# Phase boundaries of a transformer kernel: squares and gates at the eviction, a diagonal product as the turn, and k-tile pairs turned between units

## The chip, the cores and the metric

The kernel runs on one core of a Trainium2 chip. The metric is the time of one execution on the device in microseconds. A smaller number is better. The core's engines are TensorE (PE; its weight loads are PEld), VectorE (DVE), ScalarE (ACT), GpSimd (POOL) and SyncE (SP, which here only issues loads). Each engine carries out its own instructions in order, and the engines meet through semaphores.

## What is computed

Two transformer blocks on 256 latent tokens and 256 context tokens of width 2048, in fp32. The first block mixes the tokens (an mLSTM and a differential attention), projects, adds, and runs an FFN of width 5632 with a convolution over the tokens, on the latent tokens alone. The second block has two layers with two kinds of attention each; both layers read all 512 tokens, and the last updates the latent ones only. Every residual sum is followed by an RMS norm, a scale and a shift (both from a modulation row that is itself a product of a vector with a large matrix), and a product with a large weight matrix. What matters here is the chain from one large product to the next:

```python
def first_block(...):
    mod = jax.nn.silu(c) @ w_mod[l] + b_mod[l]
    sh1, sc1, ga1, sh2, sc2, ga2 = jnp.split(mod[:, None, :], N_MOD, axis=-1)
    ...
    p_lat = modulate(rmsnorm(x, g_pre_mix[l]), sh1, sc1) @ w_in[l]
    ...
    y_lat = jnp.concatenate([m_lat, d_lat], axis=-1).astype(x.dtype) @ w_out[l]
    x = x + ga1 * rmsnorm(y_lat, g_post_mix[l])
    h_lat = modulate(rmsnorm(x, g_pre_ffn[l]), sh2, sc2)
    x = x + ga2 * rmsnorm(conv_ffn(h_lat, w_up[l], conv_ffn_w[l], conv_ffn_b[l], w_down[l]), g_post_ffn[l])
    ...
def second_block(...):
    for l in range(DEPTH_2):
        h_lat = rms_norm(x, norm_g[l]) * (1.0 + scale[:, None]) + shift[:, None]
        h_ctx = rms_norm(xc, norm_g[l]) * (1.0 + scale_c) + shift_c
        ...
        x = x + gate[:, None] * merge_groups(o_a, lat_a[3], o_b, lat_b[3], w_out[l])
        if l < DEPTH_2 - 1:
            ...
            xc = xc + gate_c * merge_groups(oc_a, ctx_a[3], oc_b, ctx_b[3], w_out[l])
    return rms_norm(x, final_g)
```

## The kernel before

**Tiles and units.** Tokens lie on the 128 partitions: tiles 0 and 1 are latent, tiles 2 and 3 context. A large product is a sequence of groups, each 512 output columns wide (a few are 288), and a group is a sequence of units of two k-tiles, 128 rows of the weight matrix each. SP loads each unit's weights, 512 KB, into one of seven raw slots (L2276). ScalarE rounds them to fp32r as w_hi (L2288), VectorE subtracts to get w_lo (L2309), in four slots of each. TensorE then makes three fp32r products for each pair of operand and weight parts (L2357 to L2359 for 512 columns, L2367 to L2369 where the FFN's up projection keeps the weights still and moves 256 token columns). Units of kind "F" are modulation sums: VectorE multiplies and accumulates 128x1024 slices of the modulation matrices (L630). They are hosted between the units of other groups and share the raw slots.

**Phases and stages.** The program is a list. `gemms` appends a phase, whose steps are the units in order; `stage` appends work that isn't a large product. `walk` runs the list on each engine. Between all entries stands `barrier`: every engine adds to a semaphore, and waits for all four. In a phase `split_and_leave` walks over the steps on ScalarE and VectorE: it makes the split of each unit and, five units after a group's last unit or at the end of the phase, the group's leave, which evacuates its PSUM banks (L852 and L860 copy, 128x512 each). There are eight banks, and a group takes two or four. `AHEAD` = 2 units of the next phase are split inside a stage (`fill`), and their loads run ahead through the raw slots.

**From product to product.** At the end of the out projection and of the FFN's down projection, `after_block` makes the residual of both latent tiles: squares of y (L1803), an rsqrt of twelve small dependent VectorE instructions (L377 to L383), gate and scale (L1812), add (L1814), and a store of x to `x_spill` in DRAM from GpSimd's queue. `norm_stage` follows: squares of X (L729), a second rsqrt, X scaled in place by its reciprocal root (L751, after the spill has read it), 16 k-tiles turned by `transpose` on TensorE against an identity (L770, into four banks in turn), and for each k-tile scale and shift per partition on ScalarE (L737), the rounding to fp32r (L718 on GpSimd for odd k, L758 on VectorE for even), and the remainder (L759). The next phase's `ready` lets TensorE start on a k-tile as soon as its remainder is there, but its first unit comes behind all transposes in TensorE's order. In the layers of the second block, `res_dve` evacuates the out projection: gate (L2151) and add (L2152), per tile, and `res_act` does nothing. Between the FFN's up and down projection stands `stage(pe=wait_prods)`, which waits for the last product of gate and value (L1875 to L1878, after the convolution L1304 and L1307). At the end `fin_act` squares the two tiles (L2183), `fin_dve` makes the rsqrt and scales (L2190), and `fin_pool` stores.

## Time and profile before

| | us |
|---|---|
| three runs | 3493.6, 3494.18, 3501.28 |
| median | 3494.18 |
| the profiled execution | 3489.78 |
| its span on the core | 3488.0 |
| TensorE busy in it | 3064.1 (88%) |
| VectorE, ScalarE, GpSimd busy | 2224.8, 1213.4, 132.5 |
| mean clock granted to TensorE | 0.938 of full |

TensorE is busy in 88% of the span, and its matmuls are recorded with overlapping ends, so a busy TensorE is not one at its peak. In a timeline row the first number is the start, the second the duration, and the bracket behind it says how long the engine had been idle and what released it; for consecutive matmuls the distance of two starts tells what one costs. The granted clock is a share of full speed: 1.0 is 2.4 GHz, 0.5 is 1.2 GHz.

### The profile page before, as it was taken

The page shows a single profiled execution, that of the slowest core. Times are in us where ns is not written, and L with a number is a line of the kernel's source. Part 1 is how long each engine was busy: PE and PEld are TensorE (multiplying, and loading weights), DVE is VectorE, ACT ScalarE, POOL GpSimd, SP SyncE. Part 2 cuts the span into 40 slices and gives each one's busy share as a digit, 9 for nine tenths or more (in the row PEclk, how much of TensorE's full clock was granted, in tenths as well). Part 3 has the DMA queues.
Part 4 walks back from the last instruction along what each step waited for, and adds up shares of the span by engine and source line. Part 5 has one row for each costly group of instructions (what it writes and reads, how often), then busy time and mean ns, then how long its engine had stood idle before and what let it go on. Part 6 is the DMA issues. An engine that isn't in the chain of part 4 may idle for free. (4 is left out here: it accounts for less than half of the span.)

```text
span 3488.0 us, 41971 instructions
## 1 busy us (share of the span) xinstructions
PE 3064.1 (88%) x16281; PEld 2532.7 (73%) x16281; DVE 2224.8 (64%) x3193; ACT 1213.4 (35%) x1751; POOL 132.5 (4%) x198
## 2 busy tenths in 40 slices
PE   5999789996969999998996999888898979978996
PEld 2587567875769999997885888666656767866665
DVE  5768545738757778876866677935347844584354
ACT  6631324313444443433334222124242133324342
POOL 1000000001010000000001000000000000000000
PEclk9999999997989999999998999889999989989998
DMA  7876034730837666667873555521205626661233
GB/s 259 290 253 224 3 106 137 250 136 1 298 125 249 220 233 237 208 227 247 267 241 129 180 175 188 181 85 37 97 1 205 207 84 207 188 209 57 97 121 103
DMA packets 255286, 589.20 MB, mean 169 GB/s; under 512 B 21945, under 2 KB 30369, under 8 KB 250480
## 3 DMA queue, kind: packets, MB, share of 16 engines
q1 hardware_dynamic: 245760, 544.54, 47.2%
q0 software_dynamic: 8928, 41.32, 3.3%
q8 instruction: 129, 2.11, 0.2%
q10 hardware_dynamic: 400, 0.66, 0.1%
q14 instruction: 69, 0.57, 0.1%
HBM read 571.72 MB, written 14.72 MB: 168 GB/s over the span
## 5 line engine op out<-in xcount | busy, mean ns | idle before, releaser
L2288 ACT ACTIVATE w_hi<-raw 128x1024 fp32r<-128x1024 f32 (+1 forms) x732 | 741.8, 1032 | 1388.9 <-PE bank L2359 765.0
L2309 DVE TENSOR_TENSOR w_lo<-raw,w_hi 128x1024 fp32r<-128x1024 f32 (+1 forms) x732 | 858.9, 1190 | 507.1 <-ACT w_hi L2288 503.8
L630 DVE SCALAR_TENSOR_TENSOR acc<-raw,sc_t,acc 128x1024 f32<-128x1024 f32 x480 | 601.0, 1279 | 51.0 <-DMA acc<-in_b_ada 32.9
L2357 PE MATMUL bank<-w_hi,l_hT_hi 128*128 128x512 f32 (+1 forms) x1056 | 399.0, 378 | 46.6 <-DVE w_lo L2309 46.1
L2367 PE MATMUL bank<-f_hT_hi,w_hi 128*128 128x256 f32 x1408 | 407.1, 289 | 29.2 <-DVE w_lo L2309 29.0
L2368 PE MATMUL bank<-f_hT_lo,w_hi 128*128 128x256 f32 x1408 | 405.6, 288 | 0.0
L2369 PE MATMUL bank<-f_hT_hi,w_lo 128*128 128x256 f32 x1408 | 405.3, 288 | 0.0
L2358 PE MATMUL bank<-w_lo,l_hT_hi 128*128 128x512 f32 (+1 forms) x1056 | 395.1, 374 | 0.0
L2359 PE MATMUL bank<-w_hi,l_hT_lo 128*128 128x512 f32 (+1 forms) x1056 | 394.7, 374 | 0.0
L2367 PEld LDWEIGHTS bank<-f_hT_hi,w_hi 128*128 128x128 f32 x1408 | 277.4, 197 | 33.9 <-DVE w_lo L2309 31.6
L2369 PEld LDWEIGHTS bank<-f_hT_hi,w_lo 128*128 128x128 f32 x1408 | 277.8, 197 | 0.0
L2368 PEld LDWEIGHTS bank<-f_hT_lo,w_hi 128*128 128x128 f32 x1408 | 277.3, 197 | 0.0
L2357 PEld LDWEIGHTS bank<-w_hi,l_hT_hi 128*128 128x128 f32 x1056 | 203.5, 193 | 89.5 <-DVE w_lo L2309 46.1
L2359 PEld LDWEIGHTS bank<-w_hi,l_hT_lo 128*128 128x128 f32 x1056 | 203.4, 193 | 33.5
L2358 PEld LDWEIGHTS bank<-w_lo,l_hT_hi 128*128 128x128 f32 x1056 | 204.0, 193 | 32.5
L2357 PE MATMUL bank<-w_hi,b_hT_hi 128*128 128x512 f32 x512 | 204.6, 400 | 20.2 <-DVE w_lo L2309 19.9
L2358 PE MATMUL bank<-w_lo,b_hT_hi 128*128 128x512 f32 x512 | 202.0, 395 | 0.0
L2359 PE MATMUL bank<-w_hi,b_hT_lo 128*128 128x512 f32 x512 | 201.6, 394 | 0.0
L2357 PE MATMUL bank<-w_hi,l_cat_hi 128*128 128x512 f32 x384 | 153.4, 399 | 11.2 <-DVE w_lo L2309 10.6
L2359 PE MATMUL bank<-w_hi,l_cat_lo 128*128 128x512 f32 x384 | 151.7, 395 | 0.0
L2358 PE MATMUL bank<-w_lo,l_cat_hi 128*128 128x512 f32 x384 | 151.7, 395 | 0.0
L2357 PE MATMUL bank<-w_hi,f_a_hi 128*128 128x512 f32 x352 | 139.6, 397 | 10.4 <-DVE w_lo L2309 10.4
(436 smaller groups left out, 4652.3 us busy)
## 6 DMA issues: line engine op xcount, KB each, us to landing
raw<-in_w_in SPq DMA_DIRECT2D x240, 512.0 KB, 4.8
raw<-in_w_mod SPq DMA_DIRECT2D x192, 512.0 KB, 5.3
raw<-in_w_ada SPq DMA_DIRECT2D x192, 512.0 KB, 4.5
raw<-in_w_up SPq DMA_DIRECT2D x176, 512.0 KB, 5.1
raw<-in_w_out SPq DMA_DIRECT2D x96, 512.0 KB, 4.9
raw<-in_w_down SPq DMA_DIRECT2D x88, 512.0 KB, 5.3
raw<-in_w_in SPq DMA_DIRECT2D x32, 288.0 KB, 3.4
raw<-in_w_ukv SPq DMA_DIRECT2D x16, 512.0 KB, 3.7
```

The source lines that it names most:

```text
L630: e.scalar_tensor_tensor(acc[a][:, :], raw[s % RAW_SLOTS][:, :], scalar, acc[a][:, :], ALU.mult, ALU.add).then_inc(fma_done, 1)
L2288: e.activation(slot(w_hi[u % SPLIT_SLOTS], g.width), slot(raw[s % RAW_SLOTS], g.width), ACT.Copy).then_inc(hi_ready, 1)
L2309: e.tensor_tensor(slot(w_lo[u % SPLIT_SLOTS], g.width), slot(raw[s % RAW_SLOTS], g.width), slot(w_hi[u % SPLIT_SLOTS], g.width).bitcast(F3 ...
L2357: e.matmul(o, xh[:, k, tok], hi[:, kk, :], start=first, stop=False)
L2358: e.matmul(o, xh[:, k, tok], lo[:, kk, :], start=False, stop=False)
L2359: mm = e.matmul(o, xl[:, k, tok], hi[:, kk, :], start=False, stop=last)
L2367: e.matmul(o, hi[:, kk, c], xh[:, k, 0:n], start=first, stop=False)
L2368: e.matmul(o, hi[:, kk, c], xl[:, k, 0:n], start=False, stop=False)
L2369: mm = e.matmul(o, lo[:, kk, c], xh[:, k, 0:n], start=False, stop=last)
```

## The change

Five places of the program change. They are the boundaries between the out projection and the FFN's up projection (A), up and down projection (B), down projection and layer 0 (C), layer 0 and layer 1 (D), and the end (E).

- **No barrier and no stage at A to D.** Two phases now follow each other directly. `fill=3` splits the next phase's first three units on ScalarE and VectorE ahead of the last group's leave, and `prev` tells TensorE of which groups of the phase before it must see the banks evacuated.
- **Gate and square at the eviction.** `gated_group` (A, C) multiplies by the gate on VectorE as it evacuates a bank, while ScalarE squares the other tile's bank into a free bank, with the sum over the row; then the two change over. `residual` makes the rsqrt, and then four halves of u times reciprocal root plus X as one instruction each, with a square of each half behind it on ScalarE. At D the squares of x ride on the eviction in `res_act`, one 512-column square for each tile and group.
- **A diagonal product as turn.** X is no longer scaled. `norm_join` writes for each tile the diagonal matrix of its reciprocal roots (`dg`, identity times a column), and TensorE multiplies X's 128x128 block with it, as a plain fp32 matmul (L744 after): the block comes out turned and scaled.
- **Pairs between units.** TensorE turns the k-tiles in eight pairs. Pairs 0, 1 and 2 stand ahead of the next phase's unit 0, and pair q from then on ahead of unit q - 2. Scale and shift, rounding and remainder of pairs 0 and 1 stand ahead of the first step, those of pair q at step q + 1 of ScalarE, GpSimd and VectorE.
- **B** has `ready_prods`: a unit of the down projection waits for its own products of gate and value instead of for all.
- **The context tokens** of layer 0 are loaded during the last group of the down projection (from its unit 11), and squared by ScalarE at its units 18 and 20.
- **Order in the layers.** The key and value group (all four tiles, 24 matmuls a unit) comes ahead of the two query groups.
- **The end.** The final gain is multiplied in at the eviction (`zf`); the reciprocal root is applied in halves of 1024 columns, tile 0 on VectorE, tile 1 on ScalarE; SP stores four pieces of 512 KB.

```diff
@@ -691,103 +707,93 @@
...
+            def turn_pe(q):
+                def pe(e):
+                    e.wait_ge(norm_x, xb + nt)
+                    for k in (2 * q, 2 * q + 1):
+                        if k >= 4:
+                            e.wait_ge(norm_aff, kb + k - 3)
+                        for t in range(nt):
+                            mm = e.matmul(banks[b0 + k % 4][:, P * t:P * t + P], X[:, t, P * k:P * k + P], dg[:, t, :],
+                                          start=True, stop=True)
+                        mm.then_inc(norm_tr, 1)
+                return pe
+            def affine_act(q):
+                def act(e):
+                    for k in (2 * q, 2 * q + 1):
+                        e.wait_ge(norm_tr, kb + k + 1)
+                        if k >= 4:
+                            e.wait_ge(norm_split, kb + k - 3)
+                        for a, b, c in segs:
+                            last = e.activation(tmp[:, k % 4, a:b], banks[b0 + k % 4][:, a:b], ACT.Identity,
+                                                bias=modv[:, v_shift, k, c:c + 1], scale=modv[:, v_scale, k, c:c + 1])
+                        last.then_inc(norm_aff, 1)
+                return act
...
+            def hooks(steps):
+                def parts(at):
+                    yield "act", 0, pre["act"]
+                    yield "dve", 0, diag_dve
+                    yield "pool", 0, pre["pool"]
+                    for q in range(KT // 2):
+                        yield "pe", at(group0, max(q - 2, 0)), turn_pe(q)
+                        later = 0 if q < 2 else at(group0, 7) + 1 if q == 7 else at(group0, q + 1)
+                        yield "act", later, affine_act(q)
+                        yield "pool", later, cast_pool(q)
+                        yield "dve", later, split_dve(q)
+                return join_hooks(steps, parts)
```

The gated group, the residual and their calls:

```diff
+        def gated_group(w, ktiles, i, lhs, u, gate, gates):
+            n = n_seen["swap"] = n_seen.get("swap", 0) + 1
+            def act(e, g):
+                for j in (1, 0):
+                    if j == 0:
+                        e.wait_ge(first_gated, n)
+                    last = e.activation(banks[g.bank + 2 + j][:, :], banks[g.bank + j][:, :], ACT.Square,
+                                        accum_out=tiny[:, 4 * j + i:4 * j + i + 1])
+                    if j == 1:
+                        last.then_inc(second_squared, 1)
+                last.then_inc(evac_act, 1)
+            def dve(e, g):
+                if i == 0:
+                    e.wait_ge(gate_landed, 16 * gates)
+                c = slice(512 * i, 512 * i + 512)
+                e.tensor_tensor(u[:, 0, c], banks[g.bank][:, :], gate[:, 0, c], ALU.mult).then_inc(first_gated, 1)
+                e.wait_ge(second_squared, n)
+                e.tensor_tensor(u[:, 1, c], banks[g.bank + 1][:, :], gate[:, 0, c], ALU.mult).then_inc(evac_dve, 1)
...
+                e.sem_inc(norm_sq, 1)
+            def dve(e):
+                e.wait_ge(evac_act, last_group.number + 1)
+                chain(e, "dve", e.reduce_sum(tiny[:, 48:50], tiny[:, 0:8].rearrange("p (t i) -> p t i", i=4), AX_X))
+                rsqrt(e, tiny[:, 48:50], tiny[:, 56:58], tiny[:, 64:66], 1.0 / D)
+                e.wait_ge(aux_landed, need)
+                for t, h in halves:
+                    c = slice(1024 * h, 1024 * h + 1024)
+                    e.scalar_tensor_tensor(out[:, t, c], u[:, t, c], tiny[:, 56 + t:57 + t], X[:, t, c],
+                                           ALU.mult, ALU.add).then_inc(norm_res, 1)
+                e.wait_ge(norm_sq, sq_now)
+                chain(e, "dve", e.reduce_sum(tiny[:, 112:114], tiny[:, 8:12].rearrange("p (t i) -> p t i", i=2), AX_X))
+                n = 2
+                if ctx_done is not None:
+                    ctx_done(e)
+                    n = 4
+                rsqrt(e, tiny[:, 112:112 + n], tiny[:, 56:56 + n], tiny[:, 64:64 + n], 1.0 / D)
 
...
         tmp3 = place("f_tmp", [P, 4, 256], W0 + 8 * KB)
-        norm_stage(X1, [], LAT_TILES, junk3, tmp3, f_hi, f_lo, V_GFFN, 3, 4, before=after1)
...
+        join1, ready1 = norm_join(gs[0], X1, 2, dg3, tmp3, f_hi, f_lo, V_GFFN, 3, 4, pre1)
+        gemms(gs, sums_post + sums_l0[0], lead=12, hooks=join1, ready=ready1, prev=gs_out[2:4], fill=3)
+        gs_up = gs
+        def ready_prods(e, k):
+            e.wait_ge(prods, k // 4 + 1)
...
+        ctx_free = 11
+        def ctx_load(e):
+            e.wait_ge(unit_used, gs_down[3].units[ctx_free - 1] + 1)
...
+        def down_hooks(steps):
+            def parts(at):
+                yield "pool", at(gs_down[3], ctx_free), ctx_load
+                yield "act", at(gs_down[3], ctx_free + 7), ctx_squares(0)
+                yield "act", at(gs_down[3], ctx_free + 9), ctx_squares(1)
+            return join_hooks(steps, parts)
+        gemms(gs_down, sums_l0[1], lead=12, tail=12, first=res2, hooks=down_hooks, ready=ready_prods, prev=gs_up[-2:], fill=3)
```

The layers, the end, and the walk:

```diff
-            gs.append(Group("A", w, KT, 1024, 512, ALL_TILES, lhs, kv_act, kv_dve))
+            gs = [Group("A", w, KT, 1024, 512, ALL_TILES, lhs, kv_act, kv_dve)]
+            gs += [proj(w, KT, 512 * i, 512, qt, lhs, lambda t, i=i: q[:, t, 512 * i:512 * i + 512]) for i in range(2)]
...
-            gemms(gs, sums_g0 + sums_l1[0] if not last else sums_g1, side=(kr_group, pre, 2 if last else 1), first=pre_pool, then=gates_stored)
+            gemms(gs, sums_g0 + sums_l1[0] if not last else sums_g1, side=(kr_group, pre, 2 if last else 1), then=gates_stored,
+                  hooks=join, ready=ready_norm, prev=prev, fill=3)
...
+            def res_act(i):
+                def act(e, g):
+                    for j, t in enumerate(g.tiles):
+                        e.wait_ge(res_out, n_res + nq * i + j + 1)
+                        chain(e, "act", e.activation(rj[:, :], Xr[:, t, 512 * i:512 * i + 512], ACT.Square,
+                                                     accum_out=tiny[:, 4 * t + i:4 * t + i + 1]))
+                    e.sem_inc(evac_act, 1)
+                return act
...
+                        e.tensor_tensor(Xr[:, t, c], Xr[:, t, c], yt[:, :], ALU.add).then_inc(res_out, 1)
+                        e.wait_ge(res_out, n_res + nq * i + j + 1)
+                    if last:
+                        for t in LAT_TILES:
+                            x_ = e.tensor_tensor(zf[:, t, c], Xr[:, t, c], fg_[:, c], ALU.mult)
+                        x_.then_inc(evac_dve, 1)
+                    else:
+                        e.sem_inc(evac_dve, 1)
                 return dve
...
+            def sums_in(e):
+                e.wait_ge(evac_act, out_group.number + 1)
+                chain(e, "dve", e.reduce_sum(tiny[:, 112:112 + nq], tiny[:, 0:4 * nq].rearrange("p (t i) -> p t i", i=4), AX_X))
+                rsqrt(e, tiny[:, 112:112 + nq], tiny[:, 56:56 + nq], tiny[:, 64:64 + nq], 1.0 / D)
...
+            def fin_dve(e):
+                sums_in(e)
+                e.tensor_scalar(tiny[:, 60:62], tiny[:, 56:58], 1.0, None, ALU.mult).then_inc(fin_out, 1)
+                for h in range(2):
+                    c = slice(1024 * h, 1024 * h + 1024)
+                    e.tensor_scalar(zf[:, 0, c], zf[:, 0, c], tiny[:, 56:57], None, ALU.mult).then_inc(fin_dve_out, 1)
+            def fin_act(e):
+                e.wait_ge(fin_out, 1)
+                for h in range(2):
+                    c = slice(1024 * h, 1024 * h + 1024)
+                    e.activation(zf[:, 1, c], zf[:, 1, c], ACT.Copy, scale=tiny[:, 61:62]).then_inc(fin_act_out, 1)
...
             for at, (g, j) in enumerate(phase.steps + [(None, 0)]):
+                if g is None and phase.fill_next is not None:
+                    split_early(e, phase.fill_next[0], split, phase.fill_next[1])
...
+            out_t = A["out"][0]
+            for h in range(2):
+                c = slice(1024 * h, 1024 * h + 1024)
+                sp.wait_ge(fin_dve_out, h + 1)
+                sp.dma_start(out_t[0:P, c], zf[:, 0, c]).then_inc(out_landed, 16)
+                sp.wait_ge(fin_act_out, h + 1)
+                sp.dma_start(out_t[P:2 * P, c], zf[:, 1, c]).then_inc(out_landed, 16)
+            sp.wait_ge(out_landed, 64)
```

How the change moves instructions shows best at three places. The first is TensorE at A, behind the last matmuls of the out projection (b_cat is the mixed input, b_X the tokens, f_hT the turned and split input of the FFN, w_hi and w_lo with a number the split slots). Before:

```order
L2358 MATMUL bank<-w_lo_76,b_cat_hi 128x512
L2359 MATMUL bank<-w_hi_72,b_cat_lo 128x512
L770 MATMUL bank<-cst,b_X 128x128 x32
L2367 MATMUL bank<-f_hT_hi,w_hi_69 128x256
L2368 MATMUL bank<-f_hT_lo,w_hi_69 128x256
L2369 MATMUL bank<-f_hT_hi,w_lo_73 128x256
```

The same place of TensorE after, with the second unit's start (w_hi_70):

```order
L2465 MATMUL bank<-w_lo_76,b_cat_hi 128x512
L2466 MATMUL bank<-w_hi_72,b_cat_lo 128x512
L744 MATMUL bank<-f_dg,b_X 128x128 x12
L2474 MATMUL bank<-f_hT_hi,w_hi_69 128x256
L2475 MATMUL bank<-f_hT_lo,w_hi_69 128x256
L2476 MATMUL bank<-f_hT_hi,w_lo_73 128x256
...
L744 MATMUL bank<-f_dg,b_X 128x128 x4
L2474 MATMUL bank<-f_hT_hi,w_hi_70 128x256
```

All 32 transposes stood ahead of the first unit; now 12 products do, and four more stand ahead of each of the next units.

The second place is VectorE at B, where the last pair of the FFN (f_val, f_gate) is convolved, multiplied and split. Before:

```order
L1307 SCALAR_TENSOR_TENSOR f_gate<-bank,vecT,f_gate 128x255
L2309 TENSOR_TENSOR w_lo_73<-raw_64,w_hi_69 128x1024
L2309 TENSOR_TENSOR w_lo_74<-raw_65,w_hi_70 128x1024
L2309 TENSOR_TENSOR w_lo_75<-raw_66,w_hi_71 128x1024
L2309 TENSOR_TENSOR w_lo_76<-raw_67,w_hi_72 128x1024
L1304 SCALAR_TENSOR_TENSOR f_val<-bank,vecT,f_val 128x255
```

VectorE at the same place after:

```order
L1312 SCALAR_TENSOR_TENSOR f_gate<-bank,vecT,f_gate 128x255
L2416 TENSOR_TENSOR w_lo_73<-raw_64,w_hi_69 128x1024
L2416 TENSOR_TENSOR w_lo_74<-raw_65,w_hi_70 128x1024
L2416 TENSOR_TENSOR w_lo_75<-raw_66,w_hi_71 128x1024
L2416 TENSOR_TENSOR w_lo_76<-raw_67,w_hi_72 128x1024
L2416 TENSOR_TENSOR w_lo_73<-raw_68,w_hi_69 128x1024
L2416 TENSOR_TENSOR w_lo_74<-raw_62,w_hi_70 128x1024
L2416 TENSOR_TENSOR w_lo_75<-raw_63,w_hi_71 128x1024
L1309 SCALAR_TENSOR_TENSOR f_val<-bank,vecT,f_val 128x255
```

Three splits, the first ones of the down projection, have moved ahead of the last leave.

The third place is ScalarE at C, where the down projection (f_y) ends and layer 0 (l_X, l_tmp) begins. Before:

```order
L2288 ACTIVATE w_hi_72<-raw_68 128x1024
L852 ACTIVATE f_y<-bank 128x512
L1803 ACTIVATE f_junk_144,tiny<-f_y 128x2048 x2
L729 ACTIVATE l_junk,tiny<-l_X 128x2048 x4
L2288 ACTIVATE w_hi_69<-raw_62 128x1024
L2288 ACTIVATE w_hi_70<-raw_63 128x1024
L737 ACTIVATE l_tmp<-bank,mod 128x256 x32
```

ScalarE at the same place after:

```order
L1952 ACTIVATE bank,tiny<-l_X 128x512 x4
L2395 ACTIVATE w_hi_71<-raw_67 128x1024
L2395 ACTIVATE w_hi_72<-raw_68 128x1024
L2395 ACTIVATE w_hi_69<-raw_62 128x1024
L2395 ACTIVATE w_hi_70<-raw_63 128x1024
L2395 ACTIVATE w_hi_71<-raw_64 128x1024
L1802 ACTIVATE bank,tiny<-bank 128x512 x2
L1830 ACTIVATE l_junk,tiny<-l_X 128x1024 x4
L756 ACTIVATE l_tmp<-bank,mod 128x256 x12
L2395 ACTIVATE w_hi_72<-raw_65 128x1024
```

The context's squares stand among the last units' splits, three splits of the next phase ahead of the leave's squares, and only three pairs' scale and shift ahead of the fourth split.

## Rows read from the trace of the kernel before

**Rows 1.** the page, clock granted to TensorE, tenths, in 40 slices
```profile
PEclk9999999997989999999998999889999989989998
```

**Rows 2.** timeline, TensorE at A: start, us, engine, operation xcount [idle before]
```profile
1004.64 7.00 PE L770 MATMUL bank<-cst,b_X 128*128 128x128 f32 x28 [26.78 <-DVE b_X L751]
...
1013.10 0.35 PE L2367 MATMUL bank<-f_hT_hi,w_hi 128*128 128x256 f32 x1 [0.26 <-DVE f_hT_lo L759]
```

**Rows 3.** timeline, ScalarE and VectorE at A
```profile
978.67 1.91 ACT L1803 ACTIVATE b_junk<-b_y 128x2048 f32<-128x2048 f32 x1 [0.17 <-DVEq L2230]
980.49 0.19 ACT L1803 ACTIVATION_READ_ACCUMULATOR b_junk<-b_y 128x1 f32 x1
...
982.89 0.17 DVE L377 TENSOR_SCALAR tiny<-tiny 128x2 f32<-128x2 f32 x1 [4.29 <-ACTq L1804]
...
985.26 2.35 DVE L1812 SCALAR_TENSOR_TENSOR b_y<-b_y,tiny,b_gate 128x2048 f32<-128x2048 f32 x1
```

**Rows 4.** timeline, GpSimd behind the transposes of A
```profile
1016.48 0.95 POOL L606 MEMSET acc<- 128x1024 f32 x1 [1.04 <-DVEq L2230]
```

**Rows 5.** timeline, TensorE at B
```profile
1587.33 0.77 PE L2357 MATMUL bank<-w_hi,f_a_hi 128*128 128x512 f32 x1 [10.44 <-DVE w_lo L2309]
...
1591.15 0.39 PE L2357 MATMUL bank<-w_hi,f_a_hi 128*128 128x512 f32 x1
```

**Rows 6.** timeline, VectorE at B
```profile
1583.34 1.23 DVE L1878 TENSOR_TENSOR f_a_lo<-f_val,f_a_hi 128x1024 fp32r<-128x1024 f32 x1
```

**Rows 7.** timeline, TensorE at C
```profile
1867.18 5.59 PE L770 MATMUL bank<-cst,l_X 128*128 128x128 f32 x32 [26.43 <-DVE l_X L751]
1873.03 0.66 PE L770 MATMUL bank<-cst,l_X 128*128 128x128 f32 x4 [0.26 <-ACT l_tmp L737]
...
1880.40 0.47 PE L2357 MATMUL bank<-w_hi,l_hT_hi 128*128 128x512 f32 x1 [0.26 <-DVE l_hT_lo L759]
```

**Rows 8.** timeline, VectorE and TensorE at D
```profile
2842.27 0.69 DVE L2152 TENSOR_TENSOR l_Xr<-l_Xr,l_yt 128x512 f32<-128x512 f32 x1
...
2858.70 7.42 PE L770 MATMUL bank<-cst,l_Xr 128*128 128x128 f32 x40 [21.54 <-DVE l_Xr L751]
...
2871.93 0.47 PE L2357 MATMUL bank<-w_hi,l_hT_hi 128*128 128x512 f32 x1 [0.26 <-DVE l_hT_lo L759]
...
2880.46 0.47 PE L2357 MATMUL bank<-w_hi,l_hT_hi 128*128 128x512 f32 x1 [2.83 <-DVE w_lo L2309]
...
2884.64 0.39 PE L2359 MATMUL bank<-w_hi,l_hT_lo 128*128 128x512 f32 x1
```

**Rows 9.** windows (two at C): length, busy (x) by engine, clock, DMA, GB/s
```profile
1867.00:1871.00 4.00, 3.82 (x19) 3.85 (x20) 3.42 (x5) 2.70 (x6) 0.68 (x1) 0.52 0.41 121
1871.00:1880.00 9.00, 6.88 (x48) 4.74 (x45) 8.34 (x13) 8.86 (x20) 3.95 (x5) 1.00 0.20 64
...
1565.00:1575.00 10.00, 10.00 (x86) 10.00 (x85) 1.71 (x2) 1.06 (x1) 0.00 (x0) 1.00 0.57 203
1600.00:1612.00 12.00, 12.00 (x54) 9.94 (x53) 4.90 (x4) 5.07 (x5) 0.00 (x0) 1.00 0.83 288
```

**Rows 10.** timeline, TensorE in the attention of layer 1
```profile
3340.21 1.06 PE L948 MATMUL bank<-l_kvm,l_mPT 128*128 128x128 f32 x8
```

**Rows 11.** groups of VectorE by form: xcount, busy us, mean ns, idle before
```profile
L2309 DVE TENSOR_TENSOR w_lo<-raw,w_hi 128x1024 fp32r<-128x1024 f32 x692 | 833.3, 1222 | 474.5 <-ACT w_hi L2288 471.2 <-DVE l_ckv_kr L434 0.2 <-PE bank L2359 0.2
L630 DVE SCALAR_TENSOR_TENSOR acc<-raw,sc_t,acc 128x1024 f32<-128x1024 f32 x480 | 601.0, 1279 | 51.0 <-DMA acc<-in_b_ada 32.9 <-DMA acc<-in_b_mod 10.4 <-DVE f_gate L1307 0.9
```

**Rows 12.** groups of ScalarE by form
```profile
L2288 ACT ACTIVATE w_hi<-raw 128x1024 fp32r<-128x1024 f32 x692 | 718.2, 1057 | 1308.8 <-PE bank L2359 709.6 <-PE bank L2369 302.7 <-DMA raw<-in_w_in 165.2
```

**Rows 13.** window over eight of layer 1's short units
```profile
2894.00:2916.00 22.00, 22.00 (x99) 18.23 (x98) 15.18 (x14) 9.11 (x10) 0.00 (x0) 1.00 0.89 292
```

**Rows 14.** timeline, VectorE at E
```profile
3458.83 0.69 DVE L2151 TENSOR_TENSOR l_yt<-bank,l_gate 128x512 f32<-128x512 f32 x1 [8.50 <-PE bank L2359]
```

**Rows 15.** windows at the end of the last stores
```profile
3477.00:3478.00 1.00, 0.00 (x0) 0.00 (x0) 0.00 (x0) 0.00 (x0) 0.00 (x0) 0.50 0.54 221
```

More of the change, by code:

```diff
@@ L317, in number_units, with gemms @@
                     counted[which] += 1
[L319 removed]
+        def gemms(mains, sums=(), lead=8, tail=3, rest=4, side=None, first=None, then=None, start=(), hooks=None, hosts=None, prev=(), fill=0, ready=None):
             alone = [(g, j) for g in mains for j in range(g.n_units)]
@@ L359, in gemms @@
                 hooks = hooks(steps)
-            program.append(("gemms", None, Phase(steps, side, first, then, hooks or {})))
+            phase = Phase(steps, side, first, then, hooks or {})
+            phase.ready = ready
+            if fill:
+                program[-1][2].fill_next = (phase, fill)
+            program.append(("gemms", None, phase))
         aux = [0]
```

264 lines of the change are left out of this document (115 added, 149 removed).

## The prediction

> **What bounds the kernel now.** I read the page's row of the granted clock first, then the timeline of TensorE where that row dips, then VectorE, ScalarE and GpSimd at the same places. TensorE is the engine that all others serve, so a microsecond in which it stands is a microsecond of the kernel. The clock row [rows 1] dips between phases. The change touches five places: out projection to FFN up (A), FFN up to FFN down (B), FFN down to layer 0 (C), layer 0 to layer 1 (D), and the end (E). Let T be the end of TensorE's last matmul ahead of the boundary (a row's start less its idle time). The stop up to the first unit of the next phase is: A, T = 977.86 to 1013.10, 35.2 us [rows 2]; B, 1576.89 to 1587.33, 10.4 us [rows 5]; C, 1840.75 to 1880.40, 39.7 us [rows 7]; D, 2837.16 to 2871.93, 34.8 us, and 2.8 us more before the third unit [rows 8]. These stops are serial: the weight slots are full meanwhile and the loads stand still. So what is taken out here isn't given back, unless the next phase is short of something.
>
> The pieces inside A [rows 3]: ScalarE squares two tiles of 2048 columns from 978.67 (1.91 us, and 0.19 to read the sum), an rsqrt is twelve dependent VectorE steps, 982.89 to 985.26 (2.37 us), then gate (2.35) and add for each tile, squares again, a second rsqrt, the scaling of X (which waits for the store of x_spill to have read it), and all transposes.
>
> **A after the change.** At T gate and square of two tiles go crosswise: VectorE 0.69 for 512 columns [rows 8], ScalarE about 0.6 and 0.19 (from 1.06 for 1024 columns [rows 12] and 1.91 for 2048); two rounds, 1.5 us. A small sum and the rsqrt, 2.6. Four half-tile residuals: a 1024-column scalar_tensor_tensor is 1.28 us alone [rows 11], back to back about 1.2, so 4.8. The last half's square with its handover, 1.25 (1.06 and 0.19). Sum and rsqrt, 2.6. Two diagonals of 128 columns, 0.4. Together 13.2: the first product can start at 991.0, where the first transpose started at 1004.64.
>
> The **product** takes the place of a transpose. At full clock transposes run four in 0.66 us, 0.13 each [rows 7]. A product is a plain fp32 matmul of 128 columns; the nearest row is the attention's product with the values, where four matmuls are eight records in 1.06 us [rows 10]: (1.06 - 0.28) / 7 = 0.111 a record, so 0.22 us at full clock and 0.44 at half. I take 0.22, since shape and type are the same; the bounds are 0.13 (a transpose) and 0.52 (four of them). TensorE has idled 13 us by then and starts at half clock, as the transposes of C did: 0.52 in the first 4 us, 1.00 after [rows 9]. A turns three pairs of k-tiles ahead of its first unit: 12 products, 5.3 us, all at half clock; the split of the first pair (four products 1.8, then an affine, a cast and a split of some 0.5 each) hides behind them. First unit at 996.3, not 1013.1: 16.8 gained. The other 20 products now stand between units, 4.5 lost, and about 0.4 of the first unit is at half clock. **A: 11.9 us gained.**
>
> Do the interleaved pairs make anyone wait? TensorE turns a pair two units before it needs it, 5.8 us of matmuls in the FFN (48 at 0.12, since 85 distances fill 10.00 us) and 10.9 in the layers (48 at 0.227, 53 in 12.00 us) [rows 9]. Per step VectorE has three instructions of a pair at 0.64 (13 in 8.34 us) and 1.22 of w_lo [rows 11], ScalarE four at 0.44 (20 in 8.86 us [rows 9]) and 1.06 of w_hi, together under 3.2, against 7.2 us of TensorE in the layers and 3.8 in the FFN, where the tiles are half as wide. I cost it at nothing. GpSimd puts memsets and loads, from 1016.48 before [rows 4], between casts 2 and 3: two memsets of 0.95 and four issues, 4.5 by my estimate, where the third pair has about 7.5. The spill holds nothing any more, since X is no longer overwritten.
>
> **B.** The barrier goes, and three units of w_down are split before the last evacuation. Queued behind them on VectorE is the conv, product and split of the last FFN pair, which end at 1584.6 [rows 6], until T + 7.7. The fourth w_lo comes 1.2 later, T + 8.9; TensorE has three units of 2.72 until T + 8.2: a new stop of 0.7. Unit 20, which needs the last product, is 54 us away. The cold start goes too: nine matmuls took 1587.33 to 1591.15, 3.8 us, where nine at 0.227 take 2.0 [rows 5]. GpSimd waits for the last product as before, and its accumulator loads land at the same distance from T while the first FMA comes 12 us sooner. That FMA is still some 3 us behind them, and 8 us of split weights stand in front: nothing. **B: 10.4 + 1.8 - 0.7 = 11.5 gained.**
>
> **C.** As A, with one small sum more (2.8) and four diagonals (0.8): 13.8, the first product at 1854.5, not 1867.18. Load and squares of the context move into the down phase: two lots of four squares, 2.9 us each, on ScalarE, which has three units (8.2 us) of lead; nothing. Three pairs are 24 products, some 4.5 us of them at half clock: 7.6 (7.3 for a rise after 3.8 us, as C had it [rows 9], 8.4 for one after 6). First unit at 1862.1, not 1880.40: 18.3, less 40 products between units, 8.9. **C: 9.4 gained.**
>
> **D.** The evacuation of four tiles stays, until 2842.96 [rows 8], 5.8 us, with a square of 0.8 behind the last. Sum and rsqrt 2.6, diagonals 0.8: 10.0, first product at 2847.2, not 2858.70. First unit 7.6 later, 2854.8 instead of 2871.93: 17.1, less 8.9. Before, two short units ran out before the barrier let the splits go on: 2.83 us of stop, and then eleven matmuls in 4.18 us instead of 2.50 [rows 8]. Both go, since three units are ready and the kv group's units are twice as long: 4.5. **D: 12.7 gained.** The new order puts q0, q1 and cq, 24 short units with FMAs, in a row. Before, eight of them ran at 292 GB/s without a stop [rows 13]. At nothing, but a rival.
>
> **E.** T = 3458.8 [rows 14]. Gate and add 2.9, final gain 1.4 (the squares beside it), sum, rsqrt and handover 2.8, then the halves are scaled on two engines at once; the last is done by 3468.1. Before, the data of the stores ended at about 3477.5 [rows 15]. The same 2 MB at some 400 GB/s (221 at a share of 0.54) from 3468 end at about 3473.3. **E: 4.2 gained** (2.5 to 5.5); the 10 us behind the data stay.
>
> **Sum.** 11.9 + 11.5 + 9.4 + 12.7 + 4.2 = 49.7 us. The profiled execution took 3489.78 us, so 3440; from the median, 3494.18, which lies 4.4 higher, 3444.5.
>
> **A page that speaks against it.** The transposes ran at 0.13 us and the attention's fp32 matmuls at 0.22, a factor of 1.7. The Trainium skill (TensorE: Matmul & The Clock Gate, Terms) says that transpose mode is four times faster for fp32; by it a product would be 0.52 us, which is rival 1. The same page (Part 4: PE-mode transpose) says that transposes do not bring the clock to its full step; at C the clock stood at 1.00 from 1871 on while only transposes had run [rows 9], so the trace disagrees.
>
> **Rivals.**
> 1. No change: the product costs four transposes, 0.52 us. The 100 interleaved ones cost 29 us more, the starts of C and D 7 each and of A 3, 46 in all: 3491. Against it: the attention's row. 3%.
> 2. Slower: the pairs' lead is not there, and each of the 15 late pairs makes TensorE wait for its whole chain. It decides from 49.7 / 15 = 3.3 us a pair. The chain in the layers is eight products (1.8), four affines at 0.44, a cast and a split at 0.64, 4.8 us, and with a w_hi or w_lo in front 6: 90 us lost, 3535. For it: four in-order engines hand each pair on. Against it: the order gives each pair two units. 4%.
> 3. A moved piece shows: loads fall to 240 GB/s in D's 24 short units (292 x 22 / 8 = 803 KB a unit, so 3.35 us instead of 2.72, 15 us in all), or the first steps go at VectorE's pace. 35 us gained, 3459. 13%.
> 4. The product runs at the transposes' 0.13: 9 us between units and 5 at the starts, 3430. 6%.
>
> **Numbers.** My forecast, 3436 to 3454, has 74%. With rival 3 and what lies between, the range is 3433 to 3461. A measurement can tell about 0.2%, 7 us, from no change. Faster 93%, same 3%, slower 4%.
>
> **What would show it.** First units 18.5 (A), 21.4 (C) and 17.6 us (D) after the last matmul; at B one stop of under 1 us and no half clock; products at 0.11 a record; no wait of over 1 us ahead of units 1 to 7 of A, C and D. Wrong would make it: products of over 0.3 us, waits for hT_lo between units, or for weights in layer 1's q groups.

## The result, and the profile after

The changed kernel takes 3433.24 us (median of 4 runs, 3432.58 to 3433.55); the kernel before took 3493.89 in the same comparison (3493.27 to 3501.28). The ratio is 0.9821, with an interval of 0.9804 to 0.9838. The forecast was 3444, its own range 3436 to 3454, the whole range 3433 to 3461. The gain is 60.7 us where 49.7 were forecast: the sign is right, the size was too small, and against the median that the forecast started from, the ratio gives 3431.6, below the range. The profiled execution took 3432.58 us with a span of 3430.8, 57.2 less than the profiled execution of before.

The clock row of the page of after, to set against [rows 1]:

```profile
PEclk9999999997899999999999999989999999989999
```

The low places between phases are fewer: four digits below 9 instead of eight; the lowest is 7 in both. The span can be cut at the ends of TensorE's last matmul ahead of each boundary, T. Each line of this table is worked out from starts and durations of the two timelines of TensorE.

| us | before | after | gained | forecast |
|---|---|---|---|---|
| start to T of A | 977.9 | 976.4 | 1.4 | 0 |
| A, T to T of B | 599.0 | 588.5 | 10.5 | 11.9 |
| B, T to T of C | 263.9 | 250.9 | 13.0 | 11.5 |
| C, T to T of D | 996.4 | 989.6 | 6.9 | 9.4 |
| D, T to T of E | 621.6 | 610.9 | 10.8 | 12.7 |
| E, T to the end | 29.2 | 14.5 | 14.7 | 4.2 |

The 1.4 us of the first line are scatter: the change touches nothing there, and in the executions of this document T of A lies anywhere from 976.3 to 977.9 with the code of before, and from 975.8 to 982.4 with that of after.

TensorE at the four boundaries, the timeline of after, answering to [rows 2, 5, 7, 8] (start, us, operation, count, idle time before it and what ended it). At A, the first group of products and the first unit, and a pair between units:

```profile
989.88 5.49 PE L744 MATMUL bank<-f_dg,b_X 128*128 128x128 f32 x24 [13.44 <-DVE f_dg L735]
995.02 0.56 PE L2474 MATMUL bank<-f_hT_hi,w_hi 128*128 128x256 f32 x1
...
998.20 1.06 PE L744 MATMUL bank<-f_dg,b_X 128*128 128x128 f32 x8
999.01 0.36 PE L2474 MATMUL bank<-f_hT_hi,w_hi 128*128 128x256 f32 x1
...
1001.96 1.05 PE L744 MATMUL bank<-f_dg,b_X 128*128 128x128 f32 x8
1002.77 0.36 PE L2474 MATMUL bank<-f_hT_hi,w_hi 128*128 128x256 f32 x1
```

At B, the start of the fourth unit, with the stop ahead of it:

```profile
1573.95 0.47 PE L2464 MATMUL bank<-w_hi,f_a_hi 128*128 128x512 f32 x1 [0.78 <-DVE w_lo L2416]
```

At C and D:

```profile
1829.93 8.12 PE L744 MATMUL bank<-l_dg,l_X 128*128 128x128 f32 x48 [14.09 <-DVE l_dg L735]
1837.81 0.48 PE L2464 MATMUL bank<-w_hi,l_hT_hi 128*128 128x512 f32 x1
...
1843.37 1.95 PE L744 MATMUL bank<-l_dg,l_X 128*128 128x128 f32 x16
1845.07 0.48 PE L2464 MATMUL bank<-w_hi,l_hT_hi 128*128 128x512 f32 x1
...
1852.31 0.48 PE L2464 MATMUL bank<-w_hi,l_hT_hi 128*128 128x512 f32 x1
...
2815.71 8.44 PE L744 MATMUL bank<-l_dg,l_Xr 128*128 128x128 f32 x48 [10.32 <-DVE l_dg L735]
2823.91 0.47 PE L2464 MATMUL bank<-w_hi,l_hT_hi 128*128 128x512 f32 x1
```

The stops from T to the first unit are 18.6 us at A (T = 976.44), nothing at B, where one stop of 0.78 comes 9.0 us after T = 1564.98, 22.0 at C (T = 1815.84) and 18.5 at D (T = 2805.39). A pair of products between two units takes 0.81 from its start to the unit's at A and 1.70 at C.

At the end, the answer to [rows 14, 15]: VectorE begins at 3416.30, SyncE issues the four stores, and the data are over before 3430:

```profile
3416.30 0.69 DVE L2235 TENSOR_TENSOR l_yt<-bank,l_gate 128x512 f32<-128x512 f32 x1 [8.50 <-PE bank L2466]
...
3423.04 1.41 DVE L2269 TENSOR_SCALAR fin_z<-fin_z,tiny 128x1024 f32<-128x1024 f32 x2
...
3423.82 0.36 SPq L2383 DMA_DIRECT2D out<-fin_z  x1
...
3425.53 1.19 SPq L2385 DMA_DIRECT2D out<-fin_z  x1
...
3429.00:3430.00 1.00, 0.00 (x0) 0.00 (x0) 0.00 (x0) 0.00 (x0) 0.00 (x0) 0.50 0.87 340
3430.00:3430.80 0.80, 0.00 (x0) 0.00 (x0) 0.00 (x0) 0.00 (x0) 0.00 (x0) 0.50 0.00 0
```

The window row shows 0.87 of a microsecond of transfers behind 3429.0, so the last byte moves at 3429.9, and the span ends 0.9 us later. Before, the data ended at 3477.5 and the span at 3488.0, 10.5 us later. The ends of the data are read from such shares, which is good to some 0.3 us.

### The profile page after: what moved, and what is told of

Same layout as the page of the kernel before. It is cut to its first block and busy times, and to the rows that moved or that the text cites. A ratio compares the mean times of both kernels' runs of the same rounds, so it can differ in the third digit from the quotient of the medians.

```text
span 3430.8 us, 42418 instructions
## 1 busy us (share of the span) xinstructions
PE 3072.5 (90%) x16441; PEld 2550.2 (74%) x16441; DVE 2211.8 (64%) x3217; ACT 1222.0 (36%) x1825; POOL 127.2 (4%) x196
```

## Experiments: what ends the program

The tail is the time from the last stored byte to the end of the span. Where the prediction was most wrong is E, so four kernels change who issues the last stores and who waits for them. The kernel before, with SyncE issuing:

```diff
             def fin_pool(e):
-                for t in range(2):
-                    e.wait_ge(t_dve, bd + t + 1)
-                    aux_dmas(e, [(A["out"][0][P * t:P * t + P, :], Xf[:, t, :])])
-                e.wait_ge(aux_landed, stored_f)
+                e.wait_ge(out_landed, 32)
...
+            for t in range(2):
+                sp.wait_ge(t_dve, bd + t + 1)
+                sp.dma_start(A["out"][0][P * t:P * t + P, :], Xf[:, t, :]).then_inc(out_landed, 16)
```

> The kernel before, with one thing changed: its two last stores of 1 MB are issued by SyncE instead of GpSimd, and SyncE waits for them. The trace of before has 10.5 us between the last stored byte (3477.5) and the end of the span, the trace of the changed kernel 0.9. Theory Q (the tail belongs to stores issued from GpSimd's queue): the tail falls to about 1 us and the kernel to 3484. Rival W (the tail belongs to GpSimd as the engine that waits last): the same, 3484. Rival B (the tail is the stage's barrier or comes with pieces of 1 MB, both kept here): the tail stays near 10 us, 3494.

In this kernel, as its diff shows, GpSimd is still the engine that waits; the expectation names SyncE, which is wrong for it. So it can't tell W from B. It took 3490.80 us (ratio 1.0003, 0.9993 to 1.0013), and its end came 28.1 us after T, 1.1 earlier than in the kernel before.

> The changed kernel, with its four last stores issued by GpSimd, which waits for them too; no barrier. Q: the tail grows from 0.9 to about 10 us, 3443. W: the same, 3443. B: tail about 1 us, 3433 to 3434.

The four `sp.dma_start` of the end and their wait became four `e.dma_start` and a wait in a GpSimd hook at the phase's end. 3446.17 us.

> The changed kernel, with the four last stores issued by GpSimd, and SyncE as the engine that waits for them. Q: tail about 10 us, 3443. W: tail about 1 us, 3434.

As that one, with only `sp.wait_ge(out_landed, 64)` left on SyncE. 3436.45 us.

> The changed kernel, stores issued by SyncE as they are, but GpSimd is the engine that waits for them. Q: tail 1 us, 3433. W: tail about 10 us, 3443.

The stores as in the changed kernel, `e.wait_ge(out_landed, 64)` on GpSimd. 3441.57 us.

Windows behind the last data, of the kernel with GpSimd issuing and waiting, of the one with GpSimd issuing and SyncE waiting (with GpSimd's last issue from the timeline), and of the one with SyncE issuing and GpSimd waiting. Columns are the stretch, its length, busy time by engine, clock, DMA share, GB/s; each second row goes to the end of the span.

```profile
3436.00:3437.00 1.00, 0.00 (x0) 0.00 (x0) 0.00 (x0) 0.00 (x0) 0.00 (x0) 0.50 0.77 303
3437.00:3447.10 10.10, 0.00 (x0) 0.00 (x0) 0.00 (x0) 0.00 (x0) 0.00 (x0) 0.50 0.00 0
```

```profile
3424.29 0.53 POOL L2284 DMA_DIRECT2D out<-fin_z  x1
...
3429.00:3430.00 1.00, 0.00 (x0) 0.00 (x0) 0.00 (x0) 0.00 (x0) 0.00 (x0) 0.50 0.15 57
3430.00:3434.60 4.60, 0.00 (x0) 0.00 (x0) 0.00 (x0) 0.00 (x0) 0.00 (x0) 0.50 0.00 0
```

```profile
3429.00:3430.00 1.00, 0.00 (x0) 0.00 (x0) 0.00 (x0) 0.00 (x0) 0.00 (x0) 0.50 0.74 287
3430.00:3439.80 9.80, 0.00 (x0) 0.00 (x0) 0.00 (x0) 0.00 (x0) 0.00 (x0) 0.50 0.00 0
```

| issues, waits | tail behind the data, us | behind GpSimd's last instruction |
|---|---|---|
| before: GpSimd, GpSimd | 10.5 | 10.5 |
| before's end with SyncE, GpSimd | 10.3 | 10.3 |
| after's end with GpSimd, GpSimd | 10.3 | 10.3 |
| after's end with SyncE, GpSimd | 10.1 | 10.1 |
| after's end with GpSimd, SyncE | 5.4 | 9.8 |
| after: SyncE, SyncE | 0.9 | far behind |

The queue (Q) falls: the stores of SyncE have the tail as well when GpSimd waits. The barrier and the 1 MB pieces (B) fall too, since after's end has neither and shows 10.3. The 5.4 us fit neither Q nor W, but the last column does: GpSimd's last issue in that kernel is at 3424.3 and takes 0.5. Theory W had 3434 for that kernel and Q 3443. So a new theory, X: the program can't end earlier than some 10 us behind GpSimd's last instruction, whatever that instruction is. Three kernels test it.

> The changed kernel, with one wait more: GpSimd waits until VectorE has scaled its second half (7.9 to 8.2 us after the last matmul), and does nothing more; SyncE stores and waits as it does. Theory X (the program can end only some 10 us after GpSimd's last instruction: 10.5 in before, 10.3, 10.1 and 10.3 where GpSimd waited for the stores, 9.8 behind its last issue where it only issued): the end comes 18 us after the last matmul instead of 14.5, with the stores' data over at 13.6 as now. Rival Y (only a wait for a DMA makes GpSimd late): 14.5.

```profile
3425.82 1.41 DVE L2269 TENSOR_SCALAR fin_z<-fin_z,tiny 128x1024 f32<-128x1024 f32 x2
...
3432.00:3433.00 1.00, 0.00 (x0) 0.00 (x0) 0.00 (x0) 0.00 (x0) 0.00 (x0) 0.50 0.63 242
3433.00:3436.80 3.80, 0.00 (x0) 0.00 (x0) 0.00 (x0) 0.00 (x0) 0.00 (x0) 0.50 0.00 0
```

The only wait added is `e.wait_ge(fin_dve_out, 2)` on GpSimd. It took 3438.57 us. VectorE's second half is done at 3427.2, the data at 3432.6, and the end comes at 3436.8: 17.8 us after T (3419.03), not 14.5, 4.2 behind the data and 9.6 behind VectorE. It isn't a wait for a DMA that makes GpSimd late.

> The kernel before, with its last stores issued by SyncE and waited for by SyncE; the stage's barrier stays, which GpSimd passes when VectorE has scaled the second tile, 14.5 us after the last matmul. Theory X: the end comes 24.5 us after the last matmul (before: 29.2; with the wait on GpSimd 28.1). Rival B (the barrier holds all until the end): 28 to 29. Rival Z (nothing but the data counts once SyncE waits): 19 to 20.

It took 3485.89 us, and the end came 23.8 us after T. VectorE, whose last instruction lets GpSimd pass the barrier, is done 14.2 after T, so the end is 9.6 behind it. B and Z fall, X stands.

> The kernel before, with its last stores issued and waited for by SyncE, and without the barrier behind the last stage, so that GpSimd's last instruction is the barrier ahead of that stage, some 3 us after the last matmul; squares, rsqrt and scaling stay as they were. Theory X (GpSimd's end, 10 us behind its last instruction, is what the end of before waited for): the end comes 19 us after the last matmul (data over at 18, then 0.9), which is 10.2 of the 14.7 us that the changed kernel gained here; the shorter chain is worth the other 4.5. Rival B (a barrier or the 1 MB stores cost something of their own): over 21 us.

```diff
                     n_bar += 1
+                    if at == len(program) - 1:
+                        break
                     barrier(e, who, n_bar, wait=who != "pe" or ready is None)
```

It took 3480.84 us. The windows at the end of this kernel, whose span is 3479.0:

```profile
3477.00:3478.00 1.00, 0.00 (x0) 0.00 (x0) 0.00 (x0) 0.00 (x0) 0.00 (x0) 0.50 0.97 401
3478.00:3479.00 1.00, 0.00 (x0) 0.00 (x0) 0.00 (x0) 0.00 (x0) 0.00 (x0) 0.50 0.01 0
```

The end comes 18.7 us after T (3460.30), not 29.2. So freeing GpSimd is worth 10.5 us in the kernel before, with squares, rsqrt and scaling untouched (1.1 of them came already with the stores issued by SyncE), and the shorter chain is worth the other 4.2 of the 14.7.

The traces also hold what the 10 us are. Behind its last instruction of the program each engine runs a closing DRAIN, which the profile puts on the line that opens the program's block, L154. These are its rows (shortest, median and longest duration in ns, then first and last start) for ScalarE, VectorE and GpSimd in the kernel before, with GpSimd's two semaphore instructions behind it:

```profile
L154 ACTq DRAIN  x1: 8/8/8, 3478.3 to 3478.3; - x1
L154 DVEq DRAIN  x1: 19/19/19, 3478.4 to 3478.4; - x1
L154 POOLq DRAIN  x1: 9292/9292/9292, 3478.5 to 3478.5; - x1
L154 POOLq EVENT_SEMAPHORE  x2: 17/17/17, 3487.8 to 3487.9; - x2
```

GpSimd's takes 9.29 us, from 3478.5 to 3487.8, and the span ends 0.2 us behind it. In the kernel just tested, where GpSimd is free early:

```profile
L154 POOLq DRAIN  x1: 9133/9133/9133, 3463.4 to 3463.4; - x1
```

It takes 9.13 us there too, but is over at 3472.6, ahead of the last data, so it costs nothing. In the seven kernels in which GpSimd is late, this DRAIN takes 9.1 to 9.9 us, starts at most 1.0 us behind the data or the instruction that GpSimd waited for (beside its last issue, where it only issues), and ends 0.2 us ahead of the span's end. In the changed kernel it takes 16.3 us, from 3330.6 on, and is hidden as a whole. Why it takes this long isn't known.

## Experiments: products, pairs and order

In these kernels the distances between the T's repeat from run to run: in six profiled executions with these parts as in the changed kernel, B took 250.8 to 250.9, C 989.3 to 990.1 and D 610.8 to 610.9 us. So one execution tells 1 us there. A does not repeat: 585.6 to 593.0 in seven kernels with the same A, 588.5 in the middle. Its first unit comes 17.5 to 18.6 us after T in them and in a second execution of the changed kernel. The kernels of this section ran once each.

> The changed kernel, with all eight pairs turned, scaled and split ahead of unit 0 instead of three ahead and five between units, at A, C and D. Theory P (a product costs 0.21 to 0.22 us between units, and ahead of the first unit ScalarE's scale and shift sets the pace, about 0.6 us a k-tile at A and 0.9 at C and D): first units 24.6 us after the last matmul at A (now 18.6), 31 at C (22.0), 27.6 at D (18.5), and 4.2, 9 and 9 us less between units: 3435, almost nothing lost. Rival I (interleaving is the main part of the gain, as a pair between units costs TensorE little): 20 us lost, 3453.

```diff
-                        yield "pe", at(group0, max(q - 2, 0)), turn_pe(q)
-                        later = 0 if q < 2 else at(group0, 7) + 1 if q == 7 else at(group0, q + 1)
+                        yield "pe", 0, turn_pe(q)
+                        later = 0
```

First units 22.3, 30.9 and 27.4 us after T, C in all 989.7, D 610.8: C and D are the same as with interleaving, within 0.2 us. The whole took 3440.78, where P had 3435; of the excess over the changed kernel 3.6 lie ahead of T of A and 4.5 in A. Neither is due to the edit as far as the traces show: the kernel in which GpSimd issues and waits, whose A is that of the changed kernel, took 593.0 us in A where this one took 593.1, and from the end of the first run of units on (77.1 and 77.2 us after T) no stop of the two lies more than 0.2 us apart. Theory P holds, but for the start at A, where it had 24.6. Turning a pair between units costs TensorE just what ScalarE's pace costs it ahead of them. Interleaving, the largest part of the change in code, brings nothing.

> The changed kernel, with transposes against the identity in place of the products with the diagonal, so the tokens are turned but not scaled by their reciprocal root (that part of the computation is left out); everything else stands. Theory P (a product costs 0.22 and a transpose 0.13 at full clock): 0.09 us less for each of the 100 between units, 3 us less ahead of the first unit at A, C and D each: 18 us less in all, 3415. Rival S (fp32 data costs the same in both, and the step of 0.13 came from something else): no change, 3433.

The unit's distance with a pair in it falls from 3.76 to 3.31 us at A and from 7.24 to 6.35 at C: 0.11 less for each of the 4 and 8. Less the unit's own 24 matmuls (2.88 and 5.45 us), the pair is left with 0.88 and 1.79 us, so a product is 0.22 and a transpose 0.11 at full clock, a factor of 2, and a product costs what the attention's row said. It took 3422.72 us in all, where P had 3415. Starts came 2.1, 2.8 and 3.4 us earlier. D was 8.9 us shorter. C wasn't, though its input projection ended 9.4 us earlier: the attention of layer 0, with the same instructions, took longer. Windows of 40 us in it, of the changed kernel and of this one:

```profile
2520.00:2560.00 40.00, 37.80 (x212) 24.76 (x211) 16.38 (x56) 17.17 (x46) 0.00 (x0) 1.00 0.00 1
```

```profile
2510.00:2550.00 40.00, 37.80 (x176) 23.57 (x176) 13.75 (x45) 14.48 (x35) 0.00 (x0) 0.85 0.00 0
```

The granted clock is 1.00 in the changed kernel and 0.85 in this one; TensorE is busy for 37.80 us in both, with 176 matmuls instead of 212. Why it fell there isn't settled (the data differ too, since they aren't scaled).

> The changed kernel with the old order of groups in both layers, the two query groups ahead of keys and values (the query evacuations then wait for the spill to have read x, long over by then). Theory N (the order is worth nothing with three units split ahead): C and D within 1 us of the changed kernel, 3433. Rival K (the longer units were what took away D's two early stops of 2.83 and 1.7 us, and the 24 short units in a row cost nothing): D 4.5 us longer, C 2 to 4, 3440. Rival 3 of the prediction (the 24 short units in a row are short of loads): D and C get faster, 3428.

C 989.8, D 610.8, in all 3436.12 (the excess over N's 3433 lies in A and ahead of it): theory N. The order of the groups is worth nothing, neither as a gain (K) nor as a loss (rival 3). The 2.83 us stop of D is gone with the old order as well.

> The changed kernel without the three early splits of the next phase (fill 0) at A to D. Theory F (B's gain is the splits that stand ahead of the convolution): at B the first w_lo comes behind 7.7 us of VectorE work, a stop of about 9 us and the half clock again, 9 to 10 us more; at A, C and D the first split stands behind the residual and the first pairs, 1 to 3 us each. 3448. Rival G (the barriers themselves were the cost at B): B's stop stays under 2 us, 3438.

B took 261.7 us, 10.8 more, with a stop of 9.0 at T. The starts of A, C and D came 1.6, 2.2 and 2.2 later; C was 3.2 and D 3.2 us longer. In all it took 3455.97, 8 more than F had; 6.2 us of the loss lie in A and ahead of it, where executions differ. Theory F.

> The changed kernel, but at B every unit of the first group of the down projection waits for the last product of gate and value, as the stage did, instead of for its own. Theory F (both halves are needed: splits ahead of the convolution, and a first unit that doesn't wait for it): the last product is there 8 us after the last matmul, so a stop of about 8 us and a start at half clock come back, B 9 to 10 us longer, 3442. Rival G2 (the early splits alone bring the gain): B within 2 us of 250.9.

B took 257.8, 6.9 more where F had 9 to 10, with a stop of 7.9; in all 3438.80. So at B both halves are needed: splits ahead of the convolution, and units that wait for their own products only.

## Experiments: the half clock at the starts

The products ahead of unit 0 ran at these clocks in the changed kernel, at A, C and D:

```profile
989.90:995.00 5.10, 5.10 (x24) 5.10 (x25) 2.07 (x6) 2.70 (x5) 1.07 (x3) 0.50 0.43 177
1829.90:1837.80 7.90, 7.87 (x48) 7.87 (x49) 2.93 (x5) 4.43 (x10) 1.00 (x2) 0.67 0.44 100
2815.70:2823.90 8.20, 8.19 (x48) 8.19 (x49) 2.93 (x5) 4.56 (x10) 1.03 (x2) 0.64 0.52 132
```

> The changed kernel with throwaway matmuls of 512 columns (a weight half of the next unit with itself, into a bank that the next phase overwrites) on TensorE ahead of the first products: 20 at A and 22 at C from the second half of the residual on, 23 at D from the second tile of the last eviction on. Theory H (the first products are slow because TensorE comes from standing still: 24 products take 7.9 us at C where a pace of two scale-and-shifts a k-tile allows about 5.4): the first units come 2.5 us earlier at A, C and D each, C's stop 19.5 for 22.0, D's 16.0 for 18.5, A's 16.1 for 18.6: 3426. Rival R (ScalarE and the split set the pace of the first pairs, whatever the clock): stops as before within 0.5 us, 3433 to 3434, or later where the throwaway work overruns.

```diff
+                    if q == 0:
+                        trigger, count, n = pre["warm"]
+                        u = group0.units[0]
+                        e.wait_ge(hi_ready, u + 1)
+                        e.wait_ge(trigger, count)
+                        hot = slot(w_hi[u % SPLIT_SLOTS], group0.width)
+                        for _ in range(n):
+                            e.matmul(banks[group0.bank][:, :], hot[:, 0, 0:P], hot[:, 0, :], start=True, stop=True)
                     e.wait_ge(norm_x, xb + nt)
```

3428.00 us (median of 4, 3426.67 to 3432.65). The stops were 16.9, 20.0 and 15.7 us, where H had 16.1, 19.5 and 16.0 and R 18.6, 22.0 and 18.5: theory H. The weight is on C and D, since the stop of A lies between 17.5 and 18.6 without throwaway matmuls too.

> The throwaway matmuls with numbers that end when the diagonals are ready: 17 at A, 20 at C, 23 at D (before 20, 22, 23; the trace showed them 0.7 and 0.6 us too long at A and C, and 0.4 us too short at D). Theory H: A's stop 16.2 (16.9), C's 19.4 (20.0), D's 15.7: 1.3 us less than with the first numbers. Rival: the clock falls back or hasn't risen with fewer, and the stops are those of the changed kernel, 18.6 and 22.0.

TensorE at C and D in this second version (L746 the throwaway matmuls, L752 the 24 products, 48 records):

```profile
1821.77 7.63 PE L746 MATMUL bank<-w_hi 128*128 128x512 f32 x20 [6.78 <-DVE l_X L1849]
1829.25 5.52 PE L752 MATMUL bank<-l_dg,l_X 128*128 128x128 f32 x48
...
2801.26 8.35 PE L746 MATMUL bank<-w_hi 128*128 128x512 f32 x23 [3.05 <-DVE l_Xr L2244]
2809.45 5.52 PE L752 MATMUL bank<-l_dg,l_Xr 128*128 128x128 f32 x48
```

The 24 products take 5.52 us in place of 8.12 and 8.44. The stops were 16.6, 19.5 and 16.5, where H had 16.2, 19.4 and 15.7; D's throwaway matmuls took 8.35 us, where the same 23 had taken 6.89, so they now ended too late. In all 3421.51 us (median of 4, 3419.12 to 3427.20).

> The changed kernel once more, beside its version with throwaway matmuls on the same chip. What A, C and D show from run to run: B, C and D the same within 0.3 us, A between 585 and 593. Its median 5 to 7 us above that of the version with throwaway matmuls.

3434.69 us (3434.17 to 3441.80) on the same chip; B, C and D were 250.8, 990.1 and 610.9, and A 588.7 with a stop of 17.5. So the throwaway matmuls are worth 13.2 us in the median, where 5 to 7 were expected: the starts gave 0.9, 2.7 and 2.0, but A was 2.4, C 6.9 and D 3.4 us shorter. The rest comes behind the starts; what brings it there wasn't isolated. The version with throwaway matmuls is the fastest kernel here, 0.9794 of before (0.9775 to 0.9814).

## Why the prediction was right, and where it failed

**The step that failed is the last sentence on E**: "the 10 us behind the data stay". I took them for a fixed cost of ending a program. They are the price of GpSimd's last instruction being late, and the change took GpSimd out of the end twice over, by its stores and by its barrier. That is 10.5 us. The chain itself was forecast at 4.2, and the kernel before with GpSimd freed, beside the changed kernel, gives 18.7 - 14.5 = 4.2. That the two agree to a tenth is in part chance: the data were to end 14.5 us after T and ended after 13.6, and 1.1 of the 10.5 comes with SyncE's issuing alone.

With that term in, the sum would have been 60.2 and the forecast 3434. That this lies within 1 us of the 3433.24 measured is luck. From one profiled execution to the other 57.2 us were gained, 7.5 more than forecast: E gave 10.5 more, B 1.5 and the part ahead of A 1.4; C gave 2.5 less, D 1.9 and A 1.4. The median adds 3.7, as shown below.

**The starts** came close to what was worked out: 18.6 us for 18.5 at A, 22.0 for 21.4 at C, 18.5 for 17.6 at D (of its 0.9, 0.3 lie ahead of the first product and 0.6 in the 24 products, 8.2 for 7.6); B's stop 0.78 for 0.7. The product was taken at 0.22 with bounds of 0.13 and 0.52; it is 0.22 in the layers and in the FFN. Rivals 1 and 4 fall, and rival 2 with them: TensorE didn't wait 0.2 us ahead of any of the units 1 to 7 of A, C and D. Rival 3 falls with the old order of groups. That kernel also corrects a reason: of the two given for D's 4.5 us, three units ready and longer units, the first is enough. The factor between product and transpose is 2.0, not the four that the Trainium skill states (TensorE: Matmul & The Clock Gate, Terms) and by which rival 1 was priced. The clock also stood at 0.50 all through A's products, as I had assumed, in the profiled execution; in the second execution of the changed kernel the same products took 4.05 us up to the first unit instead of 5.14.

**Much of what is missing from C and D, and of what is too much at B, is the clock** behind stops that I hadn't touched. Windows over the same matmuls of before and after, first the stretch behind layer 1's input projection, then the third run of units in layer 0, then the end of the up projection, then a turn of sums in the down projection. Of before:

```profile
3159.80:3221.80 62.00, 47.77 (x277) 35.42 (x277) 29.46 (x84) 31.53 (x65) 0.75 (x1) 0.92 0.03 9
2081.80:2176.90 95.10, 90.08 (x483) 78.20 (x483) 74.20 (x81) 21.50 (x27) 3.84 (x6) 1.00 0.59 188
1549.20:1576.90 27.70, 27.69 (x218) 27.48 (x217) 10.75 (x15) 7.84 (x10) 0.00 (x0) 0.94 0.36 117
1698.10:1702.60 4.50, 4.50 (x34) 4.50 (x32) 0.00 (x0) 1.06 (x1) 0.00 (x0) 0.73 0.44 139
```

Of after:

```profile
3115.10:3178.40 63.30, 49.08 (x277) 36.13 (x277) 29.59 (x84) 31.55 (x65) 0.75 (x1) 0.85 0.03 9
2048.20:2145.00 96.80, 91.64 (x484) 79.72 (x482) 74.18 (x81) 21.44 (x27) 3.84 (x6) 0.98 0.59 184
1536.60:1565.00 28.40, 28.40 (x218) 28.40 (x219) 14.43 (x18) 11.03 (x13) 0.00 (x0) 0.91 0.50 149
1674.90:1678.20 3.30, 3.30 (x31) 3.30 (x32) 0.00 (x0) 1.06 (x1) 0.00 (x0) 1.00 0.61 182
```

The same matmuls took 1.3 us more at a clock of 0.85 for 0.92 (D), 1.7 more at 0.98 for 1.00 (C, 1.6 of it in busy time), 0.7 more at 0.91 for 0.94 (A), and 1.2 less at 1.00 for 0.73 (B). So of the 2.5 us that C lacks, 1.7 lie here and 0.6 in its start; of D's 1.9, 1.3 and 0.9 (0.3 came back elsewhere); of B's 1.5 too many, 1.2 lie here. No step of my sum had a term for it, plus or minus. That the shift of the work by some microseconds is what changed the clock wasn't tried; the rows show the clock and the times.

**A and the median.** A took 599.0 us in the profiled execution of before, but 602.0, 602.1 and 603.3 in three other executions whose A was the same code. After, the middle is 588.5, which is the profiled one's. So the profiled execution of before was 3 us short in A by chance, which is most of the 4.4 us by which it lay under its median, and A gained 13.5 rather than 10.5 in the middle of the runs. I had carried the 4.4 over to the changed kernel, whose profiled execution lies only 0.7 under its median. That took 3.7 us off the forecast gain.

**What brought the gain at A, C and D** isn't the interleaving, nor the order of groups (both nothing). The early splits are worth 3.2 us at C and at D. The stop of C had been 26.4 us of idle time up to the first transpose and is now 14.1 to the first product; what the eviction, the halves and the missing scaling bring of that together was measured, but not one by one.

## What to carry to other kernels

Cut the span at the ends of the same matmuls in both traces before explaining a difference: most pieces repeat to some tenths of a microsecond where the total wanders by 10. Look at what GpSimd does last, and have it done some 10 us before the data are out: its closing DRAIN took 9 us or more in every kernel here. And where TensorE has idled and work is about to come, matmuls that nobody needs can buy the full clock for those that somebody does.

## What the runs showed of the hardware

- The span ended 9.6 to 10.5 us behind GpSimd's last instruction in seven kernels (behind the last data, where that instruction waited for them), and 0.9 to 1.0 us behind the last data where GpSimd had been done long before. 9.1 to 9.9 us of this are GpSimd's closing DRAIN; ScalarE's and VectorE's took 0.01 and 0.02 us in the kernel before.
- A plain fp32 matmul of 128 columns cost 0.22 us and a transpose in its place 0.11 at full clock.
- 24 such products took 5.5 us behind 20 or 23 throwaway matmuls, and 8.1 to 8.4 where TensorE had stood still for 14.1 and 10.3 us.
- With TensorE busy the same 37.80 us in 40, the granted clock was 1.00 in one run (212 matmuls) and 0.85 in another (176). The time of A differed by up to 7.4 us between executions of the same code, that of B and D by 0.2; C of before was 996.4 to 996.5 in three executions and 993.6 in a fourth.
